# Retrieval in two phases: all u rows first, then V half by dense tiles and half by gathered half rows

## What is computed

```
q = (x @ w_query)                       # 8 heads, two halves of 128
s1, s2 = q_half @ sub_keys              # 128 keys per half
v1, i1 = top_k(s1, 16); v2, i2 = top_k(s2, 16)
top_s, sel = top_k(v1 + v2 pairs, 16)   # 16 experts of 128*128 per head
gate = softmax(top_s)
pre = einsum('td,thkd->thk', x, expert_u[idx])
act = gelu(pre) * gate
out = einsum('thk,thkd->td', act, expert_v[idx])
```

## Time and profile before

| what | value |
|---|---|
| median of three runs | 3515.52 us |
| profiled execution, span from first to last instruction | 3509.4 us |
| TensorE busy | 2837.4 us, 81% |
| VectorE busy | 2215.7 us, 63% |
| ScalarE busy | 761.4 us, 22% |
| GpSimd busy | 1214.5 us, 35% |
| moved by DMA | 1245.00 MB, mean 355 GB/s |

### The profile page before, as it was taken

One profiled execution on the slowest core, in us unless ns is written; L12 is line 12 of the kernel. 1 busy time (PEld: TensorE's weight loads), 2 busy tenths in 40 slices (PEclk: granted clock), 3 DMA queues, 4 the chain that ended last, 5 costly groups with the idle time before them and its releaser, 6 DMA issues.

```text
span 3509.4 us, 30590 instructions
## 1 busy us (share of the span) xinstructions
PE 2837.4 (81%) x10259; PEld 1622.9 (46%) x10259; DVE 2215.7 (63%) x3120; ACT 761.4 (22%) x1198; POOL 1214.5 (35%) x1028
## 2 busy tenths in 40 slices
PE   8999848877887788777789998588778778877776
PEld 7878733423433343232389787234234333432322
DVE  6776676565655666665567766766556566656655
ACT  5455411111111111111144553111111111111111
POOL 0000154444444444443300001544444444544442
PEclk9999979999999999999999999799999999999999
DMA  5546599999999999999945465999999999999998
GB/s 192 167 138 210 187 389 422 419 421 421 420 420 420 420 413 412 422 420 419 407 135 168 144 216 203 384 421 419 422 418 419 420 421 420 417 417 421 421 422 345
DMA packets 240482, 1245.00 MB, mean 355 GB/s; under 512 B 24344, under 2 KB 36832, under 8 KB 108256
## 3 DMA queue, kind: packets, MB, share of 16 engines
q0 software_dynamic: 147456, 1073.81, 74.0%
q1 hardware_dynamic: 92896, 169.49, 14.2%
HBM read 1241.12 MB, written 2.10 MB: 354 GB/s over the span
## 4 chain that ended last, share of the span: by engine, by line
DMA 45%; PE 42%; DVE 6%; issue 4%; POOL 1%; ACT 1%; DVEq 1%; POOLq 0%; SPq 0%
DMA work<-in_peer_v_dram,idx_v 40%; PE PS L521 21%; PE PS L860 18%; DMA work<-in_peer_u_dram,idx_u 5%; DVE work L1955 2%; DVE xs L1981 1%; POOL work L1270 1%; PE PS L577 0%; DVE lo L1406 0%; PE PS L642 0%; DMA raw<-in_w_in_dram 0%; PE PS L619 0%; PE PS L796 0%; PE PS L504 0%; DVE lo L1762 0%
## 5 line engine op out<-in xcount | busy, mean ns | idle before, releaser
L860 PE MATMUL PS<-work,diag 128*128 128x512 f32 x3968 | 1862.4, 617 | 609.1 <-DMA work<-in_peer_v_dram,idx_v 440.7
L1955 DVE CUSTOM_DVE_ANT_0 work<-work,hn 128x2048 f32<-128x2048 f32 x512 | 1170.7, 2292 | 816.9 <-DMA work<-in_peer_u_dram,idx_u 811.1
L860 PEld LDWEIGHTS PS<-work,diag 128*128 128x128 f32 x3968 | 741.6, 195 | 1700.2 <-issue 1287.1
L1270 POOL DMA_INDIRECT work<-in_peer_u_dram,idx_u x512 | 650.9, 1271 | 1113.3 <-DVEq L1911 851.9
L1270 POOL DMA_INDIRECT work<-in_peer_v_dram,idx_v x512 | 563.4, 1100 | 1151.4 <-PE PS L860 985.9
L1202 ACT ACTIVATE diag<-cst,act_k 128x128 f32<-128x128 f32 x496 | 185.5, 398 | 1207.6 <-PE PS L860 1199.8
L521 PE MATMUL PS<-hT_hi,hi 128*128 128x256 f32 x960 | 285.6, 297 | 20.2 <-DVE lo L1762 15.5
L521 PE MATMUL PS<-hi,hT_hi 128*128 128x512 f32 (+1 forms) x704 | 273.6, 389 | 3.5 <-DVE lo L1406 3.5
L521 PE MATMUL PS<-hT_lo,hi 128*128 128x256 f32 x960 | 274.0, 285 | 0.0
L521 PE MATMUL PS<-hT_hi,lo 128*128 128x256 f32 x960 | 273.8, 285 | 0.0
L521 PE MATMUL PS<-hi,hT_lo 128*128 128x512 f32 (+1 forms) x704 | 267.7, 380 | 0.0
(11 more groups left out here) (287 smaller groups left out, 1676.4 us busy)
## 6 DMA issues: line engine op xcount, KB each, us to landing
raw<-in_w_in_dram SPq DMA_DIRECT2D x40, 1024.0 KB, 5.0
gain<-in_w_in_dram SPq DMA_DIRECT2D x38, 1024.0 KB, 5.0
raw<-in_peer_query_dram SPq DMA_DIRECT2D x22, 1024.0 KB, 16.1
raw<-in_w_out_dram SPq DMA_DIRECT2D x16, 1024.0 KB, 5.1
gain<-in_w_out_dram SPq DMA_DIRECT2D x16, 1024.0 KB, 5.1
work<-in_peer_query_dram SPq DMA_DIRECT2D x16, 512.0 KB, 7.1
work<-in_peer_u_dram,idx_u POOLq DMA_INDIRECT x512, 16.4
work<-in_peer_v_dram,idx_v POOLq DMA_INDIRECT x512, 15.3
```

The costliest lines, as they stand in the source:

```text
L860: mm = pe.matmul(PS[:, j, :], diag[:, n % RING, :], vrow[n % RING][:, j * 512:(j + 1) * 512], start=(k == 0), stop=(k == (TOPK - 2 if last ...
L1270: pool.indirect_dma_start(out=dst, out_offset=None, in_=tables[table], in_offset=bass.IndirectOffsetOnAxis(ap=idx, axis=0)).then_inc(loade ...
L1955: dve.tensor_tensor_reduce(r, r, hn[:, b, :], 1.0, 0.0, ALU.mult, ALU.add, pre[:, b, k:k + 1]).then_inc(u_free.sem, 1)
```

## The change

All 256 u rows of a layer are now fetched and dotted first (groups ordered block 0, then block 1, with a ring of six full rows). The picks' activations, gates and key indices are kept for a whole block (`pre`, `tops`, `i12`). Then V is taken in two halves of its columns:

- Columns 0 to 1023 ("dense"): for each block an activation matrix `A[b]` of 128 x 128 x 128 is built, where entry (j, i, t) is the summed activation of expert 128 i + j for token t. TensorE builds it for four tokens at a time from two one-hot matrices (`build`), the one-hots for block 0 by ScalarE (`make_hot` of ScalarE, during the dots of block 1), those for block 1 by VectorE (`make_hot` of VectorE, after the dots); ScalarE copies the result out of PSUM (`evict`). Then all 128 tiles of 128 rows x 1024 columns of V are loaded in order by SyncE (`load_tile`, ring of six), and `dense` multiplies each by `A[b][:, i, :]`, two matmuls of 512 columns per block.
- Columns 1024 to 2047 ("half rows"): GpSimd gathers for each pick 128 half rows of 4 KB (`fetch_v`, ring of four), and VectorE adds them, scaled, to `xs` (`add_row`), 256 per layer.

`A[0]` lies over the weight buffers, `A[1]` over the buffers of the u rows, and the dense product starts when both are complete. The matmuls with diagonals, the diagonals, `take_sum` and the copies of the indices are gone. The first block's residual is now finished after the last half row of the second block, and the next layer's `normalise` of block 0 with it.

The diff, cut to its core:

```diff
-VECTOR_ROWS = TOPK // 2
-U_ROWS = GROUPS * TOPK + VECTOR_ROWS
-V_ROWS = GROUPS * TOPK - VECTOR_ROWS
-U_TURNS, V_TURNS = U_ROWS // RING - 1, V_ROWS // RING
-LAST_V = (GROUPS - 1) * TOPK
+PICKS = HEADS * TOPK
+URING, VRING, TILES = 6, 4, 6
+U_ROWS, V_ROWS = GROUPS * TOPK, GROUPS * TOPK
+U_SLOT = [len(range(i, U_ROWS, URING)) for i in range(URING)]
+TILE_SLOT = [len(range(i, NKEYS, TILES)) for i in range(TILES)]
+DENSE = D // 2
...
+        urow = [region(a * D, D) for a in (0, 1, 2, 3, 4, 6)]
...
+        A = [late[:, 0:NKEYS * P].rearrange("p (i t) -> p i t", i=NKEYS), work[:].rearrange("p (i t) -> p i t", i=NKEYS)]
+        vrow = [late[:, NKEYS * P + i * DENSE:NKEYS * P + (i + 1) * DENSE] for i in range(VRING)]
+        vtile = [late[:, NKEYS * P + (VRING + i) * DENSE:NKEYS * P + (VRING + i + 1) * DENSE] for i in range(2)]
+        vtile += [hn[:, i // 2, (i % 2) * DENSE:(i % 2 + 1) * DENSE] for i in range(4)]
...
+                stop_until(sp, "sp", query_done.sem, query_done.upto(l, QPIECES))
+                load_tile(0)
+                load_tile(1)
+                stop_until(sp, "sp", dotted.sem, dotted.upto(l, 1))
+                load_tile(2)
+                load_tile(3)
+                stop_until(sp, "sp", idx_ready.sem, idx_ready.upto(l, GROUPS))
+                next_gain = norm_mix[l + 1:l + 2] if l + 1 < DEPTH else norm_final.unsqueeze(0)
+                sp.dma_start(gain[:].unsqueeze(1), next_gain.partition_broadcast(P)).then_inc(gain_loaded.sem, 16)
+                stop_until(sp, "sp", dotted.sem, dotted.upto(l, 2))
+                for i in range(4, NKEYS):
+                    load_tile(i)
...
+                    if b == 0:
+                        pe.wait_ge(hot0_ready.sem, hot0_ready.upto(l, n + 1))
+                    else:
+                        pe.wait_ge(hot1_ready.sem, hot1_ready.upto(l, n + 1))
+                    if m >= 2:
+                        pe.wait_ge(evicted.sem, evicted.upto(l, m - 1))
+                    for u in range(BATCH):
+                        mm = pe.matmul(PS[:, 6 + n % 2, u * NKEYS:(u + 1) * NKEYS], hot[:, n % 2, 0, u, :], hot[:, n % 2, 1, u, :],
+                                       start=True, stop=True)
+                    mm.then_inc(built.sem, 1)
...
+                def dense(i, b):
+                    for o in range(2):
+                        mm = pe.matmul(PS[:, 2 * b + o, :], A[b][:, i, :], vtile[i % TILES][:, o * 512:(o + 1) * 512],
+                                       start=(i == 0), stop=(i == NKEYS - 1))
+                    return mm
...
+                for b in range(NB):
+                    turn_picks(b)
+                    for n in range(NHOT):
+                        build(b, n)
+                pe.wait_ge(evicted.sem, evicted.upto(l, 2 * NHOT))
+                for i in range(NKEYS - TAIL):
+                    tile_landed(i)
+                    dense(i, 0)
+                    dense(i, 1).then_inc(tiles_used.sem, 1)
...
+                    for w, source in ((0, 2), (1, 1)):
+                        for u in range(BATCH):
+                            t = BATCH * n + u
+                            act.activation(hot[:, n % 2, w, u, :], const("iota"), ACT.Abs, bias=turned_picks[:, source, t:t + 1])
+                    act.drain()
+                    both = hot[:, n % 2].rearrange("p w u n -> p (w u n)")
+                    act.activation(both, both, ACT.Relu, bias=1.0, scale=-1.0)
+                    act.drain()
+                    for u in range(BATCH):
+                        t = BATCH * n + u
+                        a = act.activation(hot[:, n % 2, 1, u, :], hot[:, n % 2, 1, u, :], ACT.Copy, scale=turned_picks[:, 0, t:t + 1])
+                    a.then_inc(hot0_ready.sem, 1)
...
+                    stop_until(pool, "pool", v_free.sem, v_free.upto(l, r - VRING + 1))
+                    pool.indirect_dma_start(out=vrow[r % VRING], out_offset=None, in_=halves_v,
+                                            in_offset=bass.IndirectOffsetOnAxis(ap=idx[:, b, k:k + 1], axis=0)
+                                            ).then_inc(v_loaded[r % VRING].sem, 16)
+                for r in range(U_ROWS):
+                    fetch_u(r)
+                pool.wait_ge(query_done.sem, query_done.upto(l, QPIECES))
+                for r in range(V_ROWS):
+                    fetch_v(r)
...
+                def make_hot(n):
+                    dve.wait_ge(built.sem, built.upto(l, NHOT + n - 1))
+                    ts = slice(BATCH * n, BATCH * (n + 1))
+                    dve.tensor_tensor(hot[:, n % 2, 0], bc(const("iota").unsqueeze(1), [P, BATCH, NKEYS]),
+                                      bc(turned_picks[:, 2, ts].unsqueeze(2), [P, BATCH, NKEYS]), ALU.is_equal)
+                    for u in range(BATCH):
+                        t = BATCH * n + u
+                        d = dve.tensor_scalar(hot[:, n % 2, 1, u, :], const("iota"), turned_picks[:, 1, t:t + 1], turned_picks[:, 0, t:t + 1],
+                                              ALU.is_equal, ALU.mult)
+                    d.then_inc(hot1_ready.sem, 1)
+                def add_row(r):
+                    b, k = r // PICKS, r % PICKS
+                    dve.wait_ge(v_loaded[r % VRING].sem, v_loaded[r % VRING].upto(l, 16 * (r // VRING + 1)))
+                    x = xs[:, b, DENSE:D]
+                    dve.scalar_tensor_tensor(out=x, in0=vrow[r % VRING], scalar=pre[:, b, k:k + 1], in1=x, op0=ALU.mult, op1=ALU.add)
+                    d = dve.drain()
+                    d.then_inc(v_free.sem, 1)
...
+                finish_dots(1)
+                activate(1)
+                add_row(0)
+                dve.wait_ge(picks_taken.sem, picks_taken.upto(l, 2))
+                for n in range(NHOT):
+                    make_hot(n)
+                    if n % 2 == 1:
+                        add_row(n // 2 + 1)
+                for r in range(NHOT // 2 + 1, V_ROWS - 16):
...
+                dve.wait_ge(dense_done.sem, dense_done.upto(l, 1))
+                dve.tensor_tensor(xs[:, 0, 0:DENSE], xs[:, 0, 0:DENSE], bank(0, 2), ALU.add)
                 dve.drain().then_inc(x0_final.sem, 1)
-                dve.tensor_scalar(layer_base[:], layer_base[:], float(EXPERTS), None, ALU.add)
-                add_row(0)
-                add_row(1)
                 variance(0, sumsq_ready.upto(l, 2))
-                add_row(2)
                 invert(0, std_ready.upto(l, 2))
                 normalise(l + 1, 0)
-                add_row(3)
-                add_row(4)
+                dve.wait_ge(tiles_used.sem, tiles_used.upto(l, NKEYS))
+                for o in range(2):
+                    r = xs[:, 1, o * 512:(o + 1) * 512]
+                    dve.tensor_tensor(r, r, bank(2 + o), ALU.add).then_inc(x1_final.sem, 1)
```

More of the change, by code:

```diff
@@ L86 @@
 NCONST = _at
-KEPT = P + TOPK
+KEPT = P + NKEYS
 def constants():
@@ L174, in trunk @@
         hss = sb("hss", [P, NB, NH])
[L175 to L183, removed]
+        layer_base = sb("layer_base", [P, 2])
+        idx = sb("idx", [P, NB, PICKS], U32)
+        pre = sb("pre", [P, NB, PICKS])
         def const(name):
@@ L253, in trunk @@
         cand2 = tk[:, 752:1008]
[L254 to L259, removed]
+        chosen = tk[:, 1008:1520].rearrange("p (s k j) -> p s k j", s=2, k=TOPK)
         def slab_bank(g, b):
@@ L494, in _ @@
         def _(pe):
-            for s in (pieces_used, query_done, keyed):
+            for s in (pieces_used, query_done, keyed, tiles_used):
                 pe.sem_inc(s.sem, s.start)
@@ new lines, in _ @@
+                keep_scores(HEADS - 1)
+                gate_exp(0)
+                gelu(0)
+                take_picks(0)
+                make_hot(0)
+                for n in range(1, NHOT):
+                    make_hot(n)
+                    evict(0, n - 1)
+                evict(0, NHOT - 1)
+                gate_exp(1)
+                gelu(1)
+                take_picks(1)
+                for n in range(NHOT):
+                    evict(1, n)
+                act.activation(rms[:], ones[:, 0:NB], ACT.Sqrt)
@@ new lines, in _ @@
+                choose_early()
+                split_first(2)
+                dots(0, range(2))
+                split_first(3)
+                dots(0, range(2, 5))
+                split_query(0, 0)
+                dots(0, range(5, 6))
+                dots_between(0, 6)
+                dots(0, range(11, 12))
+                split_query(0, 1)
+                dots(0, range(12, 14))
+                split_query(0, 2)
+                dots(0, range(14, TOPK))
+                split_query(0, 3)
@@ new lines, in _ @@
+                for g in range(1, GROUPS):
+                    if g in (2, 4):
+                        i = g // 2
+                        dots(g, range(2))
+                        split_query(i, 0)
+                        dots_between(g, 2)
+                        split_query(i, 1)
+                        dots(g, range(7, 11))
```

(33 more changed lines are left out.)

623 lines of the change are left out of this document (283 added, 340 removed).

## The result

The changed kernel takes 3684.3 us (median of 4 runs, 3680.0 to 3691.1), the kernel before 3514.2 (3512.2 to 3516.5): a ratio of 1.0486, 95% interval 1.0474 to 1.0498. The forecast was 3600 us in 3450 to 3720, slower at 0.70. The sign and the range held; the size did not: +85 us forecast, +170 measured, twice as much.

What follows compares the result with a forecast made beforehand. VectorE was to replace DMA as the first phase's bound. 763 + 80 + 325 + 192 = 1360 us a layer against 1324, twice +36, plus 13 of tails: 3515.5 + 85 = 3600 us, range 3450 to 3720.

Steps and rivals of the forecast that it cites:

- First phase, 763 us, VectorE's: Fetching and dotting 256 u rows per layer: VectorE bounds it at 755 us plus 8 us of waits; DMA needs 664.
- Between the phases, 80 us: Last dot to first dense product, per layer: block 1's matrix is built with 16 row sums between; bounds 62 and 95.
- Pairs, 122 x 2.66 = 325 us: Dense stretch per layer: tiles and half rows share the queues one to one, 2.66 us a pair; bounds 305 and 342.
- The term for the queues: In the dense stretch, 1.33 us per 0.524 MB transfer, so a tile and a half row take 2.66 us.
- the cover: In the dense stretch, TensorE's 1.72 us a tile and VectorE's 1.35 were both taken as hidden under the transfers.
- Rows alone, 1.7 us each: After the last tile, 113 half rows per layer in a ring of four, 6.7 us a turn: 192 us, bounds 147 and 249.
- slow TensorE gives the rows the DMA: Rival for the dense stretch: clock stays at 1.2 GHz, a tile takes 3.44 us, DMA stays full; 3469 to 3527 us, chance 0.12.
- The rival of the starving ring: Rival for the half rows: the ring of four needs 2.65 us a row throughout, 3833 us in total; chance 0.09.
- The tails: Work after the last half row that was hidden before: about 8 us more in layer 0, 5 us at the end.
- The signs: Profile readings named beforehand per stretch: VectorE over 95%, DMA under 90%, gap about 80 us, then about 390 and 310 GB/s.
- the forecast's own range: Total time of the changed kernel if the main forecast holds: 3530 to 3690 us, chance 0.53.
- the two terms of the last stretch: Stretch behind the gap, per layer: 325 us for tiles paired with half rows, then 192 us for rows alone.

Runs made afterwards that it cites:

- half_dots: Changed kernel with every dot product of the first phase over 1024 of its 2048 columns, u rows still fetched whole; 3506.4 us.
- no_build1: Changed kernel without building block 1's activation matrix (no one-hots, products or evictions for it); 3602.5 us.
- half_dense: Changed kernel multiplying only columns 0 to 511 of the dense product after the first tile, all tiles and rows still fetched; 3666.5 us.
- ring6_tiles4: Changed kernel with six half-row buffers and four tile buffers in place of four and six; 3515.0 us, ratio 1.0001 to the kernel before.
- rows_alone: Changed kernel with 8 of the 128 tiles loaded and multiplied, ring of four half-row buffers kept; 3520.7 us.
- after: The changed kernel itself, nothing left out; 3684.3 us, ratio 1.0486 to the kernel before.
- rows_alone_ring6: As the changed kernel but with only 4 of the 128 tiles and six half-row buffers in place of four; 3294.9 us.

## Why the prediction was right in sign and half right in size

- **First phase, 763 us, VectorE's.** Right: 766 and 765 measured, VectorE busy 731 of 764 us, and `half_dots` shows the cause.
- **Between the phases, 80 us.** Right: 79, at 126 GB/s; by `no_build1` it is worth 46 us a layer.
- **Pairs, 122 x 2.66 = 325 us.** The term for the queues was right (2.61 us a pair in `half_dense`), the cover was not. "TensorE needs 4 x 0.43 = 1.72 us a tile" took the pitch of one record for a product. It is 0.86, a tile 3.44, and TensorE set the stretch: 441 us. The group of the v sums in the trace before, with two records for each product, could have told. In the total this cost some 13 us a layer only, because rows passed beside it. That is luck: the tile stretch grew by 116 us, and nothing in the prediction counted on rows to fill it.
- **Rows alone, 1.7 us each.** This term is the most of the miss. The landing was taken at 4.4 us from direct transfers and a least value; it is 5.5, which is most of the way from a turn of 6.7 us to one of 8.0 and from a row of 1.7 us to one of 2.0. On the forecast's own count of 113 rows that is 36 us a layer; `half_dense` has 37 in layer 0 and 29 in layer 1. That the ring starves beside the tiles as well, at 2.5 us a row, had no term in the sum at all; by `ring6_tiles4` two buffers more are worth the whole 170 us, beside the tiles and after them.
- **The rival "slow TensorE gives the rows the DMA"** (3469 to 3527 us) had the tile's 3.44 us right, though by the clock, which was at full speed. It took the rows at 1.7 us beside them; in the ring of four they took 2.5, where landings take 7.8 us because both queues work. With six buffers they take 2.06, and the kernel 3515 us, inside that rival's range.
- **The rival of the starving ring** named the mechanism and put it at 2.65 us a row everywhere. It was 2.5 beside tiles and 2.0 alone.
- **The tails**, 8 and 5 us: measured 7.3 and 5.
- **The signs.** VectorE over 95% busy in the first phase and the gap of 80 us came true. The DMA share there read 0.93, where under 90% was the sign, though by bytes (367 of 421 GB/s) it is 87%. The 390 GB/s for 325 us were 362 for 441 us, and the 310 GB/s after the last tile were 260.
- **The total.** The 3684 us lie inside the forecast's own range of 3530 to 3690, near its end. No lucky cancelling made the sum: the two terms of the last stretch were both too short, and of the first, 116 us short, only some 13 reached the total.
- The Trainium skill's formula for a gather (DMA: Bandwidth & Descriptors, "Anatomy of one DMA"), by which the sum would have come out 37 us a layer lower, does not hold here: the landings of `rows_alone` are 4.6 us at the least, where it gives 3.2.

## What to carry to other kernels

A ring delivers as many transfers in one turn as it has buffers, and the turn holds a landing that grows with what else is in the queues (5.5, 7.8 and 9.9 us here). Price it with a landing measured at that load, and count the buffers of each stream before a split into two is judged. When TensorE's price decides what covers what, divide the time of a stretch by the products that the code issues, not by the records that the trace lists. A byte saved pays only where the DMA engines are the bound: this change saved 67 MB a layer and handed the stretches to VectorE, to a gap, and to a ring too short for its queues.

## What the runs showed of the hardware

- An fp32 product of 128 x 128 by 512 columns takes 0.86 us at a granted clock of 1.00 and shows as two records (`after`: 1024 records for 512 products in 441 us).
- The mean busy share of the DMA engines read 0.97 at 362 GB/s, with four gathers in flight (`after`), and 1.03 at 407, with six (`ring6_tiles4`): a share near one is not a full queue.
- Median landings of a 0.52 MB gather: 5.5 us alone in a ring of four (`rows_alone`), 7.8 beside direct loads (`after`), 9.9 with six in flight beside them (`ring6_tiles4`).
- GpSimd's issues, one behind another beside a summing VectorE, come every 1.5 us in `rows_alone_ring6`, which held its gathers of half a megabyte at 347 GB/s with nothing else in the queues.
